# Norm and indexer projections in one block, index scores between the query projections, a later search, experts with the tokens stationary

## What is computed

```python
u = _rmsnorm(hp, ln1_g[l])
qa, ka, va, qi, ki, wi, qr, kr, vr, gr = _project(u, w_in[l], q_norm_g[l], k_norm_g[l], pos_p)
att = _dsa_prompt(qa, ka, va, qi, ki, wi, pos_p, rel_bias, k_top_prompt)
ret_o, s_fin = _retention_prompt(qr, kr, vr)
hp = hp + _merge(att, ret_o, gr, ret_gn_g[l], ret_gn_b[l], w_out[l], hp.dtype)
hp = hp + _hmoe(_rmsnorm(hp, ln2_g[l]), w_group[l], w_expert[l], w_gate[l], w_up[l], w_down[l])
...
def _index_topk(qi, wi, kidx, q_pos, k_top):
    s = jnp.einsum("bthd,bsd->bths", qi, kidx) * (IDX_DIM ** -0.5)
    score = jnp.einsum("bths,bth->bts", jax.nn.relu(s), wi)
    score = jnp.where(key_pos[None, None, :] <= q_pos[None, :, None], score, -jnp.inf)
    _, idx = lax.top_k(score, k_top)
...
h = silu(jnp.einsum("nd,edf->nef", uf, w_gate)) * jnp.einsum("nd,edf->nef", uf, w_up)
h = h * combine[:, :, None]
y = jnp.einsum("nef,efd->nd", h, w_down)
```

## Time and profile before

| | us |
|---|---|
| median of 3 runs | 1939.34 (1933.06 to 1966.86) |
| the profiled execution | 1933.82 |
| its span in the trace | 1932.0 |

### The profile page before, as it was taken

The page is one execution under the profiler, slowest core; times in us unless marked ns, Lnnn a source line. Parts: engine busy times, 40 slices in busy tenths (PEclk is TensorE's granted clock), DMA queues, the critical chain, the costliest instruction groups (busy, mean ns, idle before and its releaser), DMA issues. The chain is left out here.

```text
span 1932.0 us, 23160 instructions
## 1 busy us (share of the span) xinstructions
PE 1636.0 (85%) x8771; PEld 1006.0 (52%) x8787; DVE 759.9 (39%) x1953; ACT 525.7 (27%) x955; POOL 171.3 (9%) x226
## 2 busy tenths in 40 slices
PE   4876999999999997899958998897535999999950
PEld 3531444455545452566645665342534777777740
DVE  4072688566666639322334554010440111111104
ACT  3252466454544510344522331000200111111100
POOL 0110000000000000000022330000123000000004
PEclk7975999999988998899968998899556999999975
DMA  6250138100200105000048994951504999999827
GB/s 177 77 165 22 33 90 233 35 1 0 88 1 1 45 24 177 0 1 1 1 119 355 381 387 165 329 170 60 162 1 109 335 337 329 338 336 340 301 90 285
DMA packets 182125, 294.66 MB, mean 153 GB/s; under 512 B 37832, under 2 KB 140392, under 8 KB 173672
## 3 DMA queue, kind: packets, MB, share of 16 engines
q1 hardware_dynamic: 157072, 173.56, 29.1%
q0 software_dynamic: 21264, 106.88, 15.3%
q10 hardware_dynamic: 3696, 12.98, 1.8%
HBM read 250.15 MB, written 48.35 MB: 155 GB/s over the span
## 5 line engine op out<-in xcount | busy, mean ns | idle before, releaser
L486 PE MATMUL m_ps<-w,uT 128*128 128x512 f32 (+1 forms) x1008 | 459.9, 611 | 7.8 <-PEq L63 6.3
L486 PEld LDWEIGHTS m_ps<-w,uT 128*128 128x128 f32 (+1 forms) x1008 | 186.8, 190 | 243.5 <-issue 238.3
L1946 DVE TENSOR_TENSOR e_hT<-e_gate,e_psG 128x192 f32<-128x192 f32 x32 | 11.3, 354 | 331.4 <-ACT e_gate L1913 331.4
L1602 PE MATMUL o_ps<-o_w,k_mixT 128*128 128x512 f32 (+1 forms) x288 | 126.6, 603 | 6.1 <-DMA o_w<-in_w_out 6.1
L1888 PEld LDWEIGHTS e_psG<-e_xT,e_wg 128*128 128x128 f32 x1024 | 122.2, 196 | 16.7 <-issue 16.7
L1898 PE MATMUL e_psY<-e_wd,e_hT 128*96 128x512 f32 x256 | 117.6, 602 | 6.4 <-DVE e_hT L1946 2.7
L1888 PE MATMUL e_psG<-e_xT,e_wg 128*128 128x96 f32 x1024 | 121.7, 278 | 0.7 <-DVE e_xT L1935 0.7
L1888 PE MATMUL e_psG<-e_xT,e_wu 128*128 128x96 f32 x1024 | 119.6, 275 | 0.0
L1888 PEld LDWEIGHTS e_psG<-e_xT,e_wu 128*128 128x128 f32 x1024 | 116.9, 192 | 0.0
L1121 DVE TENSOR_SCALAR_CACHE_REDUCE mask<-sc,m_mid 128x384 bf16<-128x384 f32 (+3 forms) x128 | 109.0, 906 | 0.0
L1390 PE MATMUL s_psK<-k_identity,s_ring 128*128 128x128 f32 x512 | 79.2, 301 | 33.1 <-ACT s_kcT L1466 12.4
(11 more groups left out here) (313 smaller groups left out, 2219.1 us busy)
## 6 DMA issues: line engine op xcount, KB each, us to landing
e_wg<-in_w_gate SPq DMA_DIRECT2D x32, 1024.0 KB, 9.5
e_wu<-in_w_up SPq DMA_DIRECT2D x32, 1024.0 KB, 12.0
e_wd<-in_w_down SPq DMA_DIRECT2D x32, 1024.0 KB, 16.1
y_rows<-e_y ACTq DMA_DIRECT2D x32, 384.0 KB, 6.9
y_rows<-m_blank SPq DMA_DIRECT2D x22, 384.0 KB, 5.2
w<-in_w_in SPq DMA_DIRECT2D x8, 1024.0 KB, 7.1
w<-in_w_in SPq DMA_DIRECT2D x3, 2048.0 KB, 8.9
skew<-tab_rows SPq DMA_DIRECT2D x8, 576.0 KB
```

What stands on the lines that cost most here:

```text
L486: mm = nc.tensor.matmul(psZ[u % 3][:n, :], A["uT"][:, k, cols_of(i)], w[buffer_of(c)][:, k, :], start=(k == 0), stop=(k == KD - 1))
L1602: mm = nc.tensor.matmul(ps[:n, i % 2, half * 512:(half + 1) * 512], src, w[:, k, half * 512:(half + 1) * 512], start=(k == 0), stop=(k == ...
```

## The change

Four edits.

1. `lead` takes the place of the first `norm_and_transpose` and of `index_projection`: one loop of eleven steps, in which PE turns tile i, projects tile i − 1, turns the projection of tile i − 2 and makes a piece of the bias table. The weights are loaded behind the second tile of x.
2. `index_scores` has no block any more. It hands out a part for each engine, which `front` calls in its first nine units: five units of prompt scores in each of u = 0 to 7, the cached keys turned in u = 1, 2, 5 and 6, the ten sample parts in u = 3, 4, 7 and 8. Two PSUM banks serve the scores instead of three and two. SP's small transfers come ahead of the loads of gains and retention states.
3. The search begins at u = 9: seven iterations in the key units, and 25 instead of 18 in the retention steps, so that seven steps have two.
4. In `experts` the tokens are stationary and the 512 columns of gate and up move; the hidden values are turned on PE in two transposes; down of expert e − 1 comes behind gate/up of e and the turn of the tokens of e + 1. Gate/up and down weights have semaphores of their own.

```diff
+def lead(nc, S, A, w, tables, casts, weights, preload, spread):
...
+            for i in range(TILES):
+                if i >= 3:
+                    sp.wait_ge(xn_ready, i - 2)
+                sp.dma_start(x[:rows_of(i), i % 3, :], S["x_rows"](i)).then_inc(x_loaded[i % 3], 16)
+                if i == 1:
+                    sp.dma_start(w[:, :, :N_QI], weights).then_inc(w_loaded, 16)
...
+            for i in range(STEPS):
+                if i < TILES:
+                    turn_rows(i)
+                if i == 1:
+                    pe.wait_ge(w_loaded, 16)
+                if 0 <= i - 1 < TILES:
+                    project(i - 1)
                 if i >= 2:
+                    turn(i - 2)
+                if 3 <= i < 3 + len(cuts):
...
+                    nc.tensor.matmul(psB[:, :n], rb[:, :], hot[:, a:a + n], start=True, stop=True).then_inc(tab_ready, 1)
...
         def _(act):
+            for i in range(STEPS):
+                if i < TILES:
...
+                    nc.scalar.activation(sq[:n, :], x[:n, i % 3, :], ACT.Square, accum_out=ms[:n, i:i + 1]).then_inc(squared, 1)
+                    act.wait_ge(mean_ready, i + 1)
+                    nc.scalar.activation(rms[:n, i:i + 1], rstd[:n, i:i + 1], ACT.Sqrt).then_inc(rooted, 1)
+                if 0 <= i - 1 < TILES:
...
+                    nc.scalar.activation(z[:n, q % 2, :], psZ[q % 2][:n, :N_QI], ACT.Copy).then_inc(z_taken, 1)
+                if i >= 2:
...
+                    nc.scalar.activation(A["qiT"][:, :, cols_of(q)], psT[:, :2, :n], ACT.Copy)
+                    nc.scalar.activation(A["kiT"][:, cols_of(q)], psT[:, 2, :n], ACT.Copy).then_inc(t_taken, 1)
+                if 3 <= i < 3 + len(cuts):
...
+                    nc.scalar.activation(tab[:, a:a + n], psB[:, :n], ACT.Copy).then_inc(tab_taken, 1)
...
-    EARLY = 14
-    early_search = lambda u: range(EARLY * u // first_pass, EARLY * (u + 1) // first_pass)
-    late_search = lambda g: range(EARLY + g, EARLY + g + 1) if EARLY + g < BISECT else ()
+    EARLY = 7
+    early_search = lambda u: range(EARLY * (u - TILES) // TILES, EARLY * (u - TILES + 1) // TILES) if u >= TILES else ()
+    late_search = lambda g: range(EARLY + (BISECT - EARLY) * g // NG_, EARLY + (BISECT - EARLY) * (g + 1) // NG_)
...
+            index_sp(sp)
+            sp.wait_ge(*index_done)
+            sp.dma_start(gg, S["ret_gn_g"].to_broadcast([P, W])).then_inc(loaded, 16)
...
                 unit(u, rows_of(i), i)
                 if u:
                     turn_attention(u - 1)
+                if u < TILES:
+                    index_pe(pe, u)
...
                     nc.scalar.activation(st[:n, 2, :], st[:n, 1, :], ACT.Sqrt).then_inc(o_rooted, 1)
+                if g < NG_:
+                    for it in late_search(g)[1:]:
+                        act_count(act, it)
...
                 norm_begin(u)
+                if u < TILES:
+                    index_dve(dve, link, u)
...
-                    for it in late_search(g):
-                        count(dve, it)
+                    count(dve, late_search(g)[0])
+                    for it in late_search(g)[1:]:
+                        close_search(dve, it - 1)
+                        aim(dve, it)
                 if 0 <= g - 2 < NG_:
                     gate(g - 2)
+                if g < NG_:
+                    for it in late_search(g)[1:]:
+                        count(dve, it)
                 if is_sample(g - 2):
                     take_sample_update(g - 2, 1)
...
+    prompt_step = lambda u: range(min(5 * u, len(units)), min(5 * u + 5, len(units)))
+    part_step = {3: (0, 1, 2), 4: (3, 4), 7: (5, 6, 7), 8: (8, 9)}
...
+        for n, q in enumerate(prompt_step(u)):
+            score(q)
+            if n < len(beside):
+                turn_keys(*beside[n])
+        for m in part_step.get(u, ()):
+            score_samples(m)
+            if m:
+                sum_heads(m - 1)
...
-                for m in range(2 * K2):
-                    w = wg if m < K2 else wu
-                    f = m % K2
-                    for k in range(KD):
-                        mm = nc.tensor.matmul(psG[:, b, m * CAP:(m + 1) * CAP], w[:, j, k, f * P:(f + 1) * P], xT[:, b, k, :],
-                                              start=(k == 0), stop=(k == KD - 1), skip_group_check=True)
+                for k in range(KD):
+                    mm = nc.tensor.matmul(psG[:, b, :], xT[:, b, k, :], wgu[:, j, k, :], start=(k == 0), stop=(k == KD - 1))
                 mm.then_inc(g_ready, 1)
                 if not (isinstance(it, int) and e == NE - 1):
-                    turn(it, j + 1)
+                    turn_tokens(it, j + 1)
+                if not (first and j == 0):
+                    down(it, j)
                 pe.wait_ge(h_ready, e + 1)
...
+                for f in range(K2):
+                    mm = nc.tensor.transpose(psH[:, b, f * CAP:(f + 1) * CAP], hid[:, b, f * P:(f + 1) * P], A["identity"][:CAP, :CAP])
+                mm.then_inc(h_turned, 1)
```

More of the change, by code:

```diff
@@ L232, in turn @@
                 pe.wait_ge(nat_ready, i + 1)
-                if i >= 2:
[L234 to L243, removed]
-                for k in range(KD):
[L245 to L251, removed]
+                if i:
+                    pe.wait_ge(t_taken, i)
@@ new lines, in index_scores @@
+    parts = [(half, rr) for half in range(2) for rr in (0, 4)] + [None]
+    M_ = 2 * len(parts)
+    prompt_step = lambda u: range(min(5 * u, len(units)), min(5 * u + 5, len(units)))
+    part_step = {3: (0, 1, 2), 4: (3, 4), 7: (5, 6, 7), 8: (8, 9)}
+    finished = lambda u: [i for i in blocks if units[prompt_step(u)[-1]][0] > i >= units[prompt_step(u)[0]][0]
+                          or u == 7 and i == NT - 1] if prompt_step(u) else []
+    order = [("prompt", q) if q is not None else ("part", m) for u in range(TILES)
+             for q, m in [(q, None) for q in prompt_step(u)] + [(None, m) for m in part_step.get(u, ())]]
@@ new lines, in index_scores, with hold @@
+    place = {what: n for n, what in enumerate(order)}
+    used = 0
+    def hold(*shape):
+        nonlocal used
+        flat = held[:, used:used + int(np.prod(shape))]
+        used += int(np.prod(shape))
+        return flat
+    kxT = hold(4, 8, P).rearrange("p (b r k) -> p b r k", b=4, r=8)
+    kx = hold(2, 16, 64).rearrange("p (b r e) -> p b r e", b=2, r=16)
+    r = hold(3, 512).rearrange("p (j n) -> p j n", j=3)
+    wsum = hold(2, 512).rearrange("p (j n) -> p j n", j=2)
+    qs = hold(DB, IH, DS).rearrange("p (b h t) -> p b h t", b=DB, h=IH)
@@ new lines, in index_scores, with sp_part @@
+    ws = hold(2)
+    psS, psR = ps[:, 5:7, :], ps[:NS, 7, :]
+    s_ready, s_taken, r_used = sem("ix_ready"), sem("ix_taken"), sem("ix_used")
+    q_loaded, ws_loaded = sem("q_loaded"), sem("ws_loaded")
+    kx_loaded = [sem(f"kx_loaded{j}") for j in range(2)]
+    heads_ready, heads_weighed, row_ready, row_taken = sem("heads_ready"), sem("heads_weighed"), sem("row_ready"), sem("row_taken")
+    def sp_part(sp):
+        with nc.allow_non_contiguous_dma(reason="small pieces of the sample queries"):
+            for half in range(2):
+                for h in range(IH):
+                    sp.dma_start(qs[half * 64:half * 64 + 64, :, h, :],
+                                 A["qiT"][h % 2 * 64:h % 2 * 64 + 64, h // 2, SEQ:].rearrange("p (b t) -> p b t", b=DB)
+                                 ).then_inc(q_loaded, 16)
+            for b in range(DB):
+                for h in range(IH):
+                    row = b % 4 * 32 + h * DS
+                    sp.dma_start(ws[row:row + DS, b // 4:b // 4 + 1], A["wi"][b * DS:(b + 1) * DS, NT, h:h + 1]
+                                 ).then_inc(ws_loaded, 16)
```

542 lines of the change are left out of this document (300 added, 242 removed).

## The result

| | before | after |
|---|---|---|
| median, 12 runs each | 1936.79 us | 1945.70 us |
| lowest, highest | 1927.76, 1971.61 | 1933.67, 1950.50 |
| the profiled execution, its span | 1933.82, 1932.0 | 1942.97, 1941.2 |

The account below looks back on a forecast made before the run. The prediction took the kernel as PE-bound on average, busy 1636.0 of 1932.0 us. Its terms, +11 − 33 + 8 − 10.5 = −24.5, gave 1909.3 from the profiled execution and 1914 us on the shown median; range 1888 to 1944.

Parts of the forecast that it names:

- the sum: Whole kernel: lead +11, index scores −33, search +8, experts −10.5, together −24.5 us, giving 1914 us.
- Lead: Merged norm and projections: steps chained through ACT, 10.4 us each with the table; end about 110, +11 us (−2 to +46).
- Index scores: Scores placed between the query units: both stages take 130 us instead of 162.6, −33 us (−40 to −22).
- Search: Seven retention steps take two iterations; step 10 costs about +5.5; in all +8 us (+3 to +15).
- Experts: Expert stage: 11.25 us per expert instead of 11.64, −10.5 us in all (−14 to 0).
- the 0.12 for handovers: Expert stage: 0.12 us for handovers, counted within the 11.25 us forecast per expert.
- The two ends of the pipeline: Expert stage: the pipeline's first gap closes (−3 us) and its last, down(31) after its own transposes, opens (+4).
- A: Lead stays at 1.2 GHz from its first gap: +46 instead of +11, 1950 us; chance 0.10.
- B: Lead at 2.4 GHz, query-phase DVE waits all hidden, search +3, experts −14: −53, 1886 us; chance 0.18.
- C: Experts bound by transfers at 11.64 us each, so their change gives nothing: −14, 1925 us; chance 0.10.
- D: Doubled search makes DVE or ACT the bound of its seven steps: +33 instead of +8, about 1940 us; chance 0.05.
- the sample parts run cold: Query phase: sample parts at 1.2 GHz together with the units around them, +56, 1970 us; chance 0.02.

Follow-up runs that it names:

- ahead_busy: Changed kernel plus 92 dummy PE products before the prompt attention, with the lead's square, root and scaling one tile ahead: 1877.49 us, ratio 0.9690 to the kernel before.
- old_lead_busy: Changed kernel plus 92 dummy PE products before the prompt attention, with the old norm and projection blocks replacing the lead: 1899.45 us, ratio 0.9809 to before.

## Why the prediction was wrong

The step that failed is the sum. It held four terms, and put every other stage at nothing without a reason, as if an untouched stage kept its clock. The prompt attention did not: +27.5, from 71.7 us at 1.2 GHz where the kernel before has 12.4; with the slow clock kept away from it, the change gave −22.2. I had read its neighbours' clocks, but not this stage's; the row 777.00 to 789.40 above, 0.50 for 12.4 us with PE busy, was there to be read, and would have told that the stage enters slow and is released at some point. The rivals had the clock in the lead and in the sample parts, which the change touches; none had it where only the moment of the begin moves. Why the moment decides stays open. That the four terms came to −19.2, so near to −24.5, is partly luck: the lead and the scores fell 11 us short, the search and the experts gave 6 back.

Point by point, by the prediction's own steps:

**Lead: right in mechanism, a little short.** The chain through ACT is as described. Timeline of one step:

```profile
43.06 1.97 PE L260 MATMUL l_psX<-k_identity,l_xn 128*128 128x128 f32 x8 [3.12 <-DVE l_xn L341]
...
44.82 6.40 PE L269 MATMUL l_psZ<-w,uT 128*128 128x324 f32 x16
...
52.54 0.59 ACT L325 ACTIVATE l_tab<-l_psB 8x512 f32<-8x512 f32 x1 [0.39 <-PE l_psB L297]
53.03 1.04 ACT L307 ACTIVATE l_sq<-l_x 128x1024 f32<-128x1024 f32 x1
...
55.63 1.57 PEld L260 LDWEIGHTS l_psX<-k_identity,l_xn 128*128 128x128 f32 x8 [4.05 <-DVE l_xn L341]
```

ACT's square stands behind the table's copy, and from there to the turns it is 2.60 us (53.03 to 55.63; I had 2.61). The turns take 1.97 and the sixteen records 6.40, so part of each step runs at 1.2 GHz. The steps with a full piece of the table take 11.4 to 12.6 us, and I had 10.4 and 1.5 for the clock. The lead ends at 114.3 instead of 110; which part of the working missed these 4 us is not shown. The +11 that went into the sum does not follow from it either: 110 − 100.2 is 9.8. The Trainium skill, "TensorE: Matmul & The Clock Gate", section "Loop structure matters more than you think", sets matmuls that come back to back against matmuls that each stand behind a long DMA wait, 8 us in its sketch, and run slow. By it I had 146. The case lies between the two: waits of 3.12 us between runs of sixteen records, and a mean clock of 0.83 over the lead, since six of the nine runs start slow and end fast. That ahead_busy, without the waits, has 1.00 from 17.4 to 72.1 agrees with the page.

**Index scores: mechanism right, three terms mis-sized.** Groups by line in the query phase:

```profile
L1075 PE MATMUL m_ps<-k_mixT 64*128 64x512 f32 (+3 forms) x80 | 33.6, 567 | 2.3 <-ACT m_held L1131 2.3
...
L1110 PE MATMUL m_ps<-m_held,k_sum_heads 128*32 128x512 f32 (+1 forms) x20 | 10.6, 614 | 4.0 <-ACT sc_s L1148 3.4 <-DVE m_held L1178 0.5
L1087 PE MATMUL m_ps<-k_identity,m_held 128*128 128x128 f32 x64 | 10.5, 287 | 0.0
...
L1100 PE MATMUL m_ps<-m_held 64*32 64x512 f32 x64 | 8.6, 617 | 0.0
```

The prompt scores take 33.6 busy (I had 29), the turns of the keys 10.5 (8), the sample parts 10.6 + 8.6 and 6.2 us of waits of which half are ACT's copy of the row (21). Without slow stretches I had the phase at 126; old_lead_busy, at 0.99, has 133.4. The 4 us between that and the 137.4 here, at 0.95, go with the clock, as much as I had put. I had foreseen the waits for DVE, 0.5 us in the trace, and not those for ACT, 5.7.

**Search: right in place and size.** +6.2 in the trace (4.3 of it in the steps), +9.7 alone, +8 predicted. Step 10 in the kernel after:

```profile
538.65 1.19 PE L634 MATMUL m_ps<-m_held,m_moving 128*128 128x128 f32 x4 [9.35 <-DVE m_held L900]
```

9 to 10 us of wait were named in advance; the other waits for ACT and DVE in these steps are 0.6 us at most.

**Experts: right, gain underrated.** One expert's chain on PE:

```profile
1549.25 0.83 PE L2005 MATMUL e_psX<-k_identity,e_xg 96*128 96x96 f32 x8
1549.91 3.60 PE L2019 MATMUL e_psY<-e_wd,e_hT 128*96 128x512 f32 x8
1553.35 0.33 PE L2042 MATMUL e_psH<-k_identity,e_hid 96*128 96x96 f32 x2
1553.51 7.03 PE L2032 MATMUL e_psG<-e_wgu,e_xT 128*96 128x512 f32 x16
...
1564.65 7.03 PE L2032 MATMUL e_psG<-e_wgu,e_xT 128*96 128x512 f32 x16
```

The next one's products begin 11.14 us after those before (1553.51 to 1564.65; 11.25 predicted), and nothing waits for weights. The mis-sized part is the 0.12 for handovers, which the trace doesn't have: an expert gains 0.5 and not 0.39, which over thirty is 15 us instead of 11.5. The two ends of the pipeline came as I had put them (−2.9 and +3.5 for −3 and +4). Together −14.3 instead of −10.5.

**Rivals.** A, the nearest to the measured time (1950), was so by accident: the lead was not slow throughout. B, C and D did not occur, nor did the sample parts run cold: the query phase has a clock of 0.95.

## What to carry to other kernels

Where PE waits long ahead of a dense stage, read that stage's granted clock by itself, and put into the forecast what it costs if the stage stays at the low level: here PE was busy 67.57 of 71.7 us and stayed there. If such a stage is long, give PE some work in the wait ahead of it: here that was worth 36 us to one kernel and 5 to another with the same stage. When two loops are merged, look for the engine whose queue now holds the head of the next step behind the tail of the last, and move the head one step ahead.

## What the hardware showed that I had not expected

From the first record of the prompt attention (774.92) to the rise of the clock (843.9) PE was busy 67.57 of 69.0 us, with no gap over half a microsecond, and was granted 1.2 GHz all that time. Whether it is released early follows the begin of the stage to within some 1.3 us (held at 71.62 and released at 72.96, released at 73.42 and held at 74.67): two DVE operations (1.4 us) released one kernel, three (2.1 us) held the other. PE runs almost without a gap from the clock's last rise until its wait, and the stage behind begins at a distance from that rise that varies little within a kernel (71.62 and 71.55 us in two executions in which the stage begins 6 us apart). That fits with eleven of twelve runs of the changed kernel lying between 1942.97 and 1950.50, though only one of them was traced, and one more beside them: the hold comes back, and looks like a property of this kernel and not of one execution.
